# Weight splits one step behind their release, head sums one step later, and local tiles' buffers for the second dilated pair

## The chip, the cores and the metric
The kernel runs on one core of one Trainium2 chip. The metric is the device time of one execution in microseconds (us), from a median of three runs. TensorE (PE) does the matrix products, ScalarE (ACT) the activations and copies, VectorE (DVE) and GpSimd (POOL) the elementwise work, and SyncE (SP) only issues DMAs. Each engine has a queue of its own, in the order in which the program wrote it, with semaphore waits between the instructions; what stands behind a waiting instruction waits too.

## What is computed
Three transformer layers run in float32 over 512 tokens of width 1024 (layers two and three also carry 256 context tokens). Each has a modulation from a condition vector, a mixer and a gated feed-forward. The change concerns the first mixer, which has two kinds of attention heads on the same normalised input:

```python
qa = rms_norm(qa.reshape(b, s, NA_HEADS, HEAD_DIM), g_qa[l])       # 8 local heads, and ka
o_a = neighbourhood_attention(qa, ka, va, rpb[l])
qb = partial_rotary(rms_norm(qb.reshape(b, s, DIL_HEADS, HEAD_DIM), g_qb[l]), pos)  # 12, and kb
for g, (win, dil) in enumerate(DIL_CONFIGS):
    o_g, lse_g = dilated_window_attention(qb[:, :, sl], kb[:, :, sl], vb[:, :, sl], win, dil)
o_b = jnp.einsum('gbsh,gbshd->bshd', wts.astype(vb.dtype), jnp.stack(outs, axis=0))
merged = gate_a * (o_a @ w_proj_a[l]) + gate_b * (o_b @ w_proj_b[l])
```

The second mixer is grouped-query attention with the same kind of head norm and rotation, the third a gated recurrence.

## The kernel before
A planner in Python writes one long list of steps (`plan`), and every engine afterwards walks this list and issues its own part of each step. The order of steps is therefore the order in all queues.

**Weights.** A weight unit (`getunit`) is up to 128x1024 values, loaded by SP into one of three buffers `RAW`. Its `Split` step makes the two summands that the three-product scheme needs: ACT copies it rounded into `SHI` (line 2044), then POOL writes the remainder into `SLO` (line 2214; in the third mixer DVE does it, line 2274, at a step `SplitLow` put up to eight steps behind). `SHI` and `SLO` have three buffers too (`NSPL = 3`), so unit k can be split once unit k-3 has been read for the last time. `release(u, tok)` notes that moment and the place in the plan, `rel_at`, which is the index of the step right after the last product (`Chunk`). `with_splits` (line 370) puts the `Split` of unit k at `rel_at` of unit k-3, that is ahead of the step which follows the product. `load_order` takes a unit's place in SP's queue from the place of the split of the unit three before it, so it moves along.

**A projection job.** `na_qk(j, which)` and `dl_qk(j, g, which)` project one pair of heads: one unit, four chunks of six products each (two of the eight 128-row tiles of the input, three products each), with a yield behind each. Behind the fourth chunk comes `release`, then the square on ACT (`squared`, line 2067). The rest is a tail, which the job hands back: `headnorm` sums the squares over each head with a product on PE (line 2490), takes logarithm and exponential on ACT (2071, 2073), and multiplies on DVE (2317); for dilated heads `roped` follows with a permutation product on PE (2494), a product with the sines on DVE (2322), and cosine product and addition on POOL (2223, 2229), which writes the tile that the scores read.

**Pipelining.** `pipelined` (line 641) advances the tail of the job before by one yield after each chunk of the present one. When the present job ends, what is left of the tail before it is run through at once. A job with no chunk of its own (`after`, `qb2_cells`, `va_turned`, `dl_turned`, `dilated_loads`) ends at once, so it also drains the tail of the job in front of it, with no chunk between. `bgz` puts one tile of the modulation (a DVE reduction, line 2298) behind every fourth yield.

**Weaving.** `weave` (line 427) runs two sequences by clocks: a step of work w advances the attention's clock by (w+1)/0.6 and the dense list's by w+1, and the one that is behind goes next. A chunk counts 3072, a head sum or rotation 2048, the scores of a dilated pair 3072, its weighted sum 3584, a turn of three blocks 768. A sequence that waits for a name (`after`) takes up the other's clock when it goes on. `attention` works on pairs of items in four stages: scores of pair i, turn (transposes) of pair i-2, weighted sum of pair i-3; "na 3 done" is noted when pair 3 of the last local heads has been finished, which is two score steps into the dilated items.

**Tiles.** Local heads' projections lie in the four buffers of ring `qa`: heads j = 0 and 2 in the first two, 1 and 3 in the others. The first dilated pair has the six `qb` buffers. The second dilated pair's six tiles (`qb2`) lie over `va` and part of `qa`, and the dense list waits for them:

```python
dense += [dl_values(2), dl_qk(0, 2, "q"), dl_turned(2), dl_qk(0, 2, "k")]
dense += [after("na 3 done"), qb2_cells()]
dense += [dl_qk(1, g, w) for g in range(3) for w in "qk"]
dense += [early_gate(q, off) for q in range(2) for off in (0, 8)]
```

**Turnovers** (`turnover`, `sums`) end a layer's part: the last residual sums in halves of 256 tokens, squares and their running sum (ACT 2048, POOL 2219), then the next norm beside the first projections. There `release` comes ahead of a square.

Of the kernel before, what the change touches and what calls it, by code (L numbers as in the profile page):

```python
# [7 lines left out]
F32 = mybir.dt.float32  # L8
# [14 lines left out]
NSPL = 3  # L23
# [79 lines left out]
def seg(a, n):  # L103
    return ((a, n),)
# [137 lines left out]
def build_program(nc, t_in, out):  # L242
# [13 lines left out]
    def all_now():  # L256
        return [last[e] for e in "pavg" if e in last]
# [13 lines left out]
    def place(name, shape, dt, at):  # L271
        return nc.alloc_sbuf_tensor_at(name, shape, dt, offset=at)
# [25 lines left out]
    AR = base[0]  # L298
# [28 lines left out]
    def col(name, k=0):  # L327
        return COL[:, COLS[name][0] + k:COLS[name][0] + k + 1]


    units, adas = [], []
# [38 lines left out]
    def with_splits(steps):  # L370

        at, p = [], 0
        for u in units:
            if u.k < NSPL:
                p = first_splits[u.k]
            if u.k >= NSPL:
                p = max(p, units[u.k - NSPL].rel_at)
            assert p <= u.first_at, (u.key, p, u.first_at)
            u.split_at = p
            at.append((p, Split(u, units[u.k - NSPL].rel if u.k >= NSPL else None)))  # L380
            if u.on == "v":
                at.append((min(p + 8, u.first_at), SplitLow(u)))
        at.sort(key=lambda q: q[0])
        done, n = [], 0
        for i, st in enumerate(steps):
            while n < len(at) and at[n][0] <= i:
                done.append(at[n][1])
                n += 1
            done.append(st)
        return done  # L390
# [27 lines left out]
    def after(key):  # L418
        while key not in emitted:
            yield "wait"  # L420
# [246 lines left out]
    def headnorm(sq, bank, src, t_mm, T, gain, W, dst, t_dfree, views=None):  # L667

        s, t1 = sq
        b2 = take()  # L670
        r = W["r"].next()
        work[0] += 4 * T
        t2, t3, t4, t5 = tick("p_head"), tick("a_hln"), tick("a_hrs"), tick("v_head")
        dview, rview = views or (None, None)
        put(HNorm(s.ap[:, 0:T], b2.ap[:, 0:T], T, r.ap[:, 0:T], src, dst, dview, rview, gain, t1, b2.free, t2,
                  r.free, t3, t4, t_dfree, t5))
        s.free = [t2]
        give(b2, t3)
        r.free = [t5]
        give(bank, t5)  # L680
        return t5
# [291 lines left out]
    def marked(items, needs, name):  # L973
# [34 lines left out]
    W = arena({"va": (1, 4 * 512, F32, 4), "qa": (4, 512, F32, 4), "vb": (1, 3 * 4 * 256, F32, 4),  # L1008
               "qb": (6, 512, F32, 4), "mk": (1, 1536, F32, 4), "bi": (5, 384, F32, 4), "e": (4, 384, F32, 4),
               "f": (4, 512, F32, 4), "pt": (3, 768, F32, 4), "r": (2, 512, F32, 4), "o": (2, 128, F32, 4), "dg": (2, 128, F32, 4),  # L1010
               "m": (8, 8, F32, 4)}, [])
    qb2 = [place(f"qb2_{i}", [128, 512], F32, AR + 2048 * i)[:, :] for i in range(6)]
    oah = place("oah", [128, 4 * NT], F32R, HCh_at)
    oal = place("oal", [128, 4 * NT], F32R, HCl_at)
    obs = [[place(f"ob{n}{j}", [128, NT], F32R, XC_at + (4096, 0)[j] + 2048 * i)[:, :] for i, n in enumerate("hl")]
# [99 lines left out]
    qa_cells, qb_cells = {}, {}  # L1115

    def na_qk(j, which):
        u = getunit("w_in", ktiles(0, 8), seg(128 * j + (0 if which == "q" else 512), 128))
        b = take()
        t, = yield from proj(u, 0, [(b.ap, hl, hl_rdy, b.free)])  # L1120
        release(u, t)
        sq = squared(b.ap, t, NT, W)
        c = W["qa"].next()

        def tail():
            views = ("p (c r) -> p c r", "p (r c) -> p c r")
            yield
            c.rdy = [headnorm(sq, b, b.ap, t, NT, gq8 if which == "q" else col("gka"), W, c.ap, c.free, views)]
            qa_cells[(which, j)] = c
            yield  # L1130
            yield
            emitted.add(f"{which} {j}")

        yield
        return tail()
# [72 lines left out]
    def dl_qk(j, g, which):  # L1208
        u = getunit("w_in", ktiles(0, 8), seg((1536 if which == "q" else 1536 + 768) + 256 * g + 128 * j, 128))
        b = take()  # L1210
        t, = yield from proj(u, 0, [(b.ap, hl, hl_rdy, b.free)])
        release(u, t)
        sq = squared(b.ap, t, NT, W)

        def tail():
            yield
            c, n = qb_cells[(which, g, j)], W["f"].next()
            t5 = headnorm(sq, b, b.ap, t, NT, gqb8 if which == "q" else col("gkb"), W, n.ap, n.free)
            yield
            yield  # L1220
            c.rdy = [roped(n, t5, NT, perm1, W, c.ap, c.free, d_rope, "p (r s) -> p r s", "p (s r) -> p r s")]
            for _ in range(4):
                yield
            emitted.add(f"dilated {which} {g} {j}")

        yield
        return tail()
# [66 lines left out]
        gated[(q, off)] = (sg, t1)  # L1294
        yield

    def qb2_cells():
        na_done = all_now()
        for i, (g, w_) in enumerate([(g, w_) for g in range(3) for w_ in ("q", "k")]):
            qb_cells[(w_, g, 1)] = Cell(qb2[i], na_done)  # L1300
        return
        yield

# [5 lines left out]
    dense = []  # L1309
# [7 lines left out]
        dense += [dl_values(j)] if j < 2 else []  # L1317
    dense += [dl_qk(0, g, w) for g in range(2) for w in "qk"]
    dense += [dl_values(2), dl_qk(0, 2, "q"), dl_turned(2), dl_qk(0, 2, "k")]
    dense += [after("na 3 done"), qb2_cells()]  # L1320
    dense += [dl_qk(1, g, w) for g in range(3) for w in "qk"]
    dense += [early_gate(q, off) for q in range(2) for off in (0, 8)]
    dense += [some(bg, 32)]
    first_out = lambda it, o, t: (na_make if "t" in it else dl_make)(it, o, t)
# [106 lines left out]
    W = arena({"hh": (6, 512, F32R, 4), "hl": (6, 512, F32R, 4), "f": (4, 512, F32, 4), "r": (2, 512, F32, 4)}, blk, c_at)  # L1431
# [43 lines left out]
    for c in W["r"].cells:  # L1475
# [14 lines left out]
    W = arena({"f": (4, 512, F32, 4), "r": (2, 512, F32, 4), "hh": (2, TT, F32R, 4), "hl": (2, TT, F32R, 4),  # L1490
               "q": (2, TT, F32, 4), "k": (2, TT, F32, 4), "v": (1, 6 * 256, F32, 4), "e": (4, TT, F32, 4),
               "pt": (2, 2 * TT, F32, 4), "o": (2, 128, F32, 4), "dg": (2, 128, F32, 4), "m": (8, 8, F32, 4)}, blk, c_at)
# [88 lines left out]
    heads, dense = [], []  # L1581
# [29 lines left out]
    W = arena({"hh": (6, TT, F32R, 4), "hl": (6, TT, F32R, 4), "f": (4, TT, F32, 4), "r": (2, 512, F32, 4)}, all_now(), c_at)  # L1611
    hid = hids(W)

    def with_mask(main):
        for i, _ in enumerate(main):
            if i == 20:
# [12 lines left out]
    W = arena({"v": (1, 6 * 256, F32, 4), "xy": (4, 2 * TT, F32, 4), "kk": (2, TT, F32, 4), "q": (2, NT, F32, 4),  # L1629
               "sg": (2, NT, F32, 4), "t": (2, TT + 1, F32, 4), "ek": (1, TT + 1, F32, 4), "eq": (1, NT, F32, 4),  # L1630
               "R": (1, 2 * NT, F32, 4), "A": (1, NT, F32, 4), "kt": (1, TT + 1, F32, 4), "S": (4, 128, F32, 4),
               "f": (1, NT, F32, 4), "r": (1, NT, F32, 4), "hh": (2, NT, F32R, 4), "hl": (2, NT, F32R, 4),
               "pe": (4, 8, F32, 4), "de": (4, 8, F32, 4)}, blk)
# [329 lines left out]
    dense = []  # L1963
# [17 lines left out]
    W = arena({"hh": (6, NT, F32R, 4), "hl": (6, NT, F32R, 4), "f": (4, NT, F32, 4), "r": (2, 512, F32, 4)}, all_now())  # L1981
# [683 lines left out]
```

## Time and profile before

| | us |
|---|---|
| median of three runs | 2824.49 |
| the three runs | 2822.01 to 2826.79 |
| the profiled execution | 2823.09 |
| its span, first to last instruction | 2820.7 |
| PE busy in it | 2635.6 |
| first mixer | about 64 to 387 |
| second mixer | about 953 to 1335 |
| third mixer | about 1950 to 2412 |

The mean granted TensorE clock was 0.976 of full speed. In a timeline row stand the start, the duration, the engine and source line, the operation with output and inputs, the count, and in brackets how long the engine had been idle before it and for what. PE works through a pipeline: matmuls of 128x512 last 0.39 us each but start 0.23 us apart, so the starts are what one counts with.

### The profile page before, as it was taken

What the parts mean: (1) busy time and instruction counts of PE and PEld (TensorE: products, weight loads), DVE (VectorE), ACT (ScalarE), POOL (GpSimd) and SP (SyncE); (2) the same over time, 40 slices, a digit from 0 to 9 for tenths busy, and PEclk for the clock granted to TensorE, in tenths of its full rate; (3) what the DMA queues carried; (4) which work ended last, traced back from release to release, by engine and by line L of the source; (5) the groups of instructions that cost most, each with busy time, mean ns of one, the idle gap of its engine ahead of it and who ended that gap; (6) DMA issues with size and microseconds to landing.
All of it is one profiled execution on the core that took longest, in us unless ns stands there. A gap on an engine that the chain in (4) does not pass through costs nothing. (4 is left out here: it accounts for less than half of the span.)

```text
span 2820.7 us, 39428 instructions
## 1 busy us (share of the span) xinstructions
PE 2635.6 (93%) x15242; PEld 2204.5 (78%) x15242; DVE 1564.4 (55%) x2439; ACT 1101.7 (39%) x2033; POOL 982.2 (35%) x561
## 2 busy tenths in 40 slices
PE   5998989899999899998899999999899998899998
PEld 3765678788888767766788888888788887788887
DVE  5445247654564445656666555556768677632224
ACT  3453442332322455555412112225555546422222
POOL 2335534444544311222333232332222122344444
PEclk9998999999999999999999999999999999899999
DMA  6643224343333100001233333321111110132222
GB/s 253 217 161 135 71 84 145 127 142 132 131 134 127 37 21 20 27 27 47 75 132 135 112 113 130 117 90 43 51 51 53 53 58 34 46 104 97 97 97 75
DMA packets 81608, 267.83 MB, mean 95 GB/s; under 512 B 8720, under 2 KB 16528, under 8 KB 81424
## 3 DMA queue, kind: packets, MB, share of 16 engines
q1 hardware_dynamic: 78000, 257.59, 26.3%
q10 hardware_dynamic: 3136, 6.42, 0.6%
q8 instruction: 122, 2.00, 0.3%
q0 software_dynamic: 288, 1.31, 0.1%
q14 instruction: 62, 0.51, 0.1%
HBM read 260.57 MB, written 4.72 MB: 94 GB/s over the span
## 5 line engine op out<-in xcount | busy, mean ns | idle before, releaser
L2214 POOL TENSOR_TENSOR SLO<-RAW,SHI 128x1024 fp32r<-128x1024 f32 (+1 forms) x291 | 708.4, 2437 | 1136.4 <-ACT SHI L2044 1130.9
L2044 ACT ACTIVATE SHI<-RAW 128x1024 fp32r<-128x1024 f32 (+1 forms) x335 | 345.4, 1035 | 1031.4 <-PE PS L2484 1024.1
L2482 PE MATMUL PS<-HLh,SHI 128*128 128x512 f32 (+1 forms) x1800 | 708.8, 394 | 21.3 <-DVE HLl L2288 11.4
L2483 PE MATMUL PS<-HLl,SHI 128*128 128x512 f32 (+1 forms) x1800 | 683.2, 380 | 0.0
L2484 PE MATMUL PS<-HLh,SLO 128*128 128x512 f32 (+1 forms) x1800 | 683.0, 379 | 0.0
L2482 PEld LDWEIGHTS PS<-HLh,SHI 128*128 128x128 f32 x1800 | 344.9, 192 | 94.0 <-issue 30.4
L2484 PEld LDWEIGHTS PS<-HLh,SLO 128*128 128x128 f32 x1800 | 344.0, 191 | 64.2
L2483 PEld LDWEIGHTS PS<-HLl,SHI 128*128 128x128 f32 x1800 | 345.3, 192 | 60.6 <-issue 5.6
L2482 PE MATMUL PS<-hh,SHI 128*128 128x512 f32 (+1 forms) x1016 | 365.3, 360 | 11.9 <-DVE XL L2360 7.9
L2484 PE MATMUL PS<-hh,SLO 128*128 128x512 f32 (+1 forms) x1016 | 356.7, 351 | 0.0
L2483 PE MATMUL PS<-hl,SHI 128*128 128x512 f32 (+1 forms) x1016 | 355.0, 349 | 0.0
L2360 DVE SCALAR_TENSOR_TENSOR XL<-PS,MOD,XL 128x512 f32<-128x512 f32 (+1 forms) x328 | 211.7, 667 | 179.2 <-PE PS L2484 179.1
L2367 DVE TENSOR_TENSOR hl<-f,hh 128x512 fp32r<-128x512 f32 x88 | 165.0, 1875 | 122.8 <-ACT hh L2113 122.8
L2482 PEld LDWEIGHTS PS<-hh,SHI 128*128 128x128 f32 x1016 | 192.3, 189 | 49.7 <-issue 11.7
L2365 DVE TENSOR_TENSOR f<-f,PS 128x512 f32<-128x512 f32 x88 | 54.3, 616 | 303.7 <-PE PS L2484 285.1
L2484 PEld LDWEIGHTS PS<-hh,SLO 128*128 128x128 f32 x1016 | 192.3, 189 | 27.1
L2483 PEld LDWEIGHTS PS<-hl,SHI 128*128 128x128 f32 x1016 | 192.4, 189 | 26.5
L2482 PE MATMUL PS<-HCh,SHI 128*128 128x256 f32 x560 | 168.0, 300 | 12.1 <-POOL SLO L2214 6.1
L2298 DVE CUSTOM_DVE_ANT_0 ADA<-ADA,cb,COL 128x1024 f32<-128x1024 f32 x96 | 177.2, 1846 | 0.0
L2483 PE MATMUL PS<-HCl,SHI 128*128 128x256 f32 x560 | 162.4, 290 | 0.0
L2484 PE MATMUL PS<-HCh,SLO 128*128 128x256 f32 x560 | 162.2, 290 | 0.0
L2298 DVE CUSTOM_DVE_ANT_0 cdump<-ADA,cb,COL 128x1024 f32<-128x1024 f32 x96 | 138.1, 1439 | 12.0 <-DMA ADA<-in_k_w 12.0
(259 smaller groups left out, 3949.9 us busy)
## 6 DMA issues: line engine op xcount, KB each, us to landing
RAW<-in_k_w SPq DMA_DIRECT2D x317, 512.0 KB, 3.5
ADA<-in_k_w SPq DMA_DIRECT2D x132, 512.0 KB, 4.3
early<-in_k_w SPq DMA_DIRECT2D x12, 512.0 KB, 18.6
RAW<-in_k_w SPq DMA_DIRECT2D x18, 256.0 KB, 2.6
XL<-in_xT ACTq DMA_DIRECT2D x4, 512.0 KB, 13.7
bi<-in_k_bias SPq DMA_DIRECT2D x16, 128.0 KB, 3.8
out<-XL SPq DMA_DIRECT2D x16, 128.0 KB, 1.8
bi<-in_k_bias SPq DMA_DIRECT2D x8, 192.0 KB, 4.1
```

The costliest lines, as they stand in the source:

```text
L2044: eng.activation(u.hi, u.w, ACT.Copy).then_inc(S["a_hi"], 1)
L2214: eng.tensor_tensor(u.lo, u.w, u.hi.bitcast(F32), ALU.subtract).then_inc(S["g_lo"], 1)
L2298: eng.tensor_tensor_reduce(w if j == n - 1 else st.dump, w, c, 1.0, st.bias, ALU.mult, ALU.add, st.mod[:, j:j + 1]).then_inc(S["v_ada"], 1)
L2360: eng.scalar_tensor_tensor(out=st.x, in0=st.src, scalar=st.gate, in1=st.x, op0=ALU.mult, op1=ALU.add).then_inc(S["v_res"], 1)
L2365: eng.tensor_tensor(st.f, st.f, st.src, ALU.mult).then_inc(S["v_up"], 1)
L2367: eng.tensor_tensor(st.lo, st.f, st.hi.bitcast(F32), ALU.subtract).then_inc(S["v_ulo"], 1)
L2482: eng.matmul(st.out, lh, rh, start=st.first and j == 0, stop=False)
L2483: eng.matmul(st.out, lh, rl, start=False, stop=False)
L2484: i = eng.matmul(st.out, ll, rh, start=False, stop=st.last and j == n - 1)
```

## The change
Three parts. The `Split` of unit k goes one step behind the place where it was, but never behind its first use. The tails of `na_qk` and `dl_qk` have one more yield ahead of the head sum. The second dilated pair's tiles go, for groups 0 and 1, into the buffers of the local tiles, as soon as local heads 2 and 3 have been scored; only group 2 takes new buffers over `va`, once the local heads are done. The one wait ahead of the six jobs becomes three waits, one ahead of each group.

```diff
@@ with_splits
             if u.k >= NSPL:
-                p = max(p, units[u.k - NSPL].rel_at)
+                p = max(p, min(units[u.k - NSPL].rel_at + 1, u.first_at))
@@
-    qb2 = [place(f"qb2_{i}", [128, 512], F32, AR + 2048 * i)[:, :] for i in range(6)]
+    qb2 = [place(f"qb2_{i}", [128, 512], F32, AR + 2048 * i)[:, :] for i in range(2)]
@@ na_qk, tail (one yield more)
             yield
+            yield
              c.rdy = [headnorm(sq, b, b.ap, t, NT, gq8 if which == "q" else col("gka"), W, c.ap, c.free, views)]
@@ dl_qk, tail (one yield more)
         def tail():
+            yield
             yield
             c, n = qb_cells[(which, g, j)], W["f"].next()
@@
-    def qb2_cells():
-        na_done = all_now()
-        for i, (g, w_) in enumerate([(g, w_) for g in range(3) for w_ in ("q", "k")]):
-            qb_cells[(w_, g, 1)] = Cell(qb2[i], na_done)
+    def qb2_cells(g):
+
+        free = all_now()
+        for i, w_ in enumerate("qk"):
+            local = W["qa"].cells[2 * g + i] if g < 2 else Cell(qb2[i], free)
+            qb_cells[(w_, g, 1)] = Cell(local.ap, local.free)
@@
-    dense += [after("na 3 done"), qb2_cells()]
-    dense += [dl_qk(1, g, w) for g in range(3) for w in "qk"]
+    for g, done in enumerate(("na 2 scored", "na 3 scored", "na 3 done")):
+        dense += [after(done), qb2_cells(g)] + [dl_qk(1, g, w) for w in "qk"]
```

## Rows read from the trace of the kernel before

**Rows 1.** The page, its first part: busy time, share, instructions of each engine
```profile
PE 2635.6 (93%) x15242; PEld 2204.5 (78%) x15242; DVE 1564.4 (55%) x2439; ACT 1101.7 (39%) x2033; POOL 982.2 (35%) x561
```

**Rows 2.** PE's waits, whole span: line, releaser, total us, times, longest
```profile
PE PS L2490 <- ACT f L2067: 13.5, 8, 1.7
...
PE PS L2482 <- POOL SLO L2214: 11.7, 6, 4.0
...
PE PS L2482 <- DVE SLO L2274: 1.0, 1, 1.0
```

**Rows 3.** Timelines of ACT and PE around one drained tail
```profile
104.87 1.06 ACT L2044 ACTIVATE SHI<-RAW 128x1024 fp32r<-128x1024 f32 x1 [0.17 <-PE PS L2484]
105.83 0.58 ACT L2067 ACTIVATE f<-PS 128x512 f32<-128x512 f32 x1
107.63 0.69 ACT L2071 ACTIVATE r<-PS,SMALL 128x512 f32<-128x512 f32 x1 [1.22 <-PE PS L2490]
...
106.47 1.13 PE L2490 MATMUL PS<-f,CONST 128*128 128x512 f32 x2 [1.69 <-ACT f L2067]
```

**Rows 4.** PE's timeline where the dense list waits for "na 3 done"
```profile
250.95 0.39 PE L2484 MATMUL PS<-HLh,SLO 128*128 128x512 f32 x1
...
256.72 2.07 PE L2494 MATMUL PS<-f,CONST 128*128 128x512 f32 x2 [2.57 <-DVE f L2317]
263.30 2.93 PE L2502 MATMUL PS<-qb,qb 64*128 64x512 f32 x12 [4.51 <-POOL qb L2229]
...
273.54 0.55 PE L2509 MATMUL PS<-CONST,e 128*128 128x128 f32 x3 [1.25 <-ACT pt L2085]
```

**Rows 5.** PE and DVE timelines, a covered tail of a dilated job
```profile
329.35 1.02 PE L2490 MATMUL PS<-f,CONST 128*128 128x512 f32 x2
...
331.60 0.39 PE L2482 MATMUL PS<-HLh,SHI 128*128 128x512 f32 x1
...
332.98 1.02 PE L2494 MATMUL PS<-f,CONST 128*128 128x512 f32 x2
...
331.80 0.75 DVE L2317 SCALAR_TENSOR_TENSOR f<-PS,COL,r 128x512 f32<-128x512 f32 x1 [4.33 <-ACT r L2073]
```

**Rows 6.** ACT, POOL and PE timelines ahead of the second dilated pair's first scores
```profile
333.23 1.06 ACT L2044 ACTIVATE SHI<-RAW 128x1024 fp32r<-128x1024 f32 x1 [1.47 <-PE PS L2484]
...
338.10 2.10 POOL L2229 TENSOR_TENSOR qb<-f,r 128x512 f32<-128x512 f32 x1
...
340.25 2.93 PE L2502 MATMUL PS<-qb,qb 64*128 64x512 f32 x12 [4.86 <-POOL qb L2229]
```

**Rows 7.** PE's timeline, and granted clock (last but two column), at a drained dilated tail
```profile
243.15 1.23 PE L2494 MATMUL PS<-f,CONST 128*128 128x512 f32 x2 [2.23 <-DVE f L2317]
243.71 1.09 PE L2482 MATMUL PS<-HLh,SHI 128*128 128x512 f32 x1
...
244.00:246.00 2.00, 2.00 (x6) 0.51 1.00 327
```

**Rows 8.** POOL and PE timelines in two turnovers
```profile
918.84 1.62 POOL L2219 TENSOR_TENSOR r<-r,f 128x256 f32<-128x256 f32 x2 [1.84 <-ACT f L2048]
920.41 2.35 POOL L2214 TENSOR_TENSOR SLO<-RAW,SHI 128x1024 fp32r<-128x1024 f32 x1
...
922.82 0.39 PE L2482 MATMUL PS<-HCh,SHI 128*128 128x256 f32 x1 [2.71 <-POOL SLO L2214]
...
1920.95 0.58 PE L2482 MATMUL PS<-HCh,SHI 128*128 128x256 f32 x1 [3.36 <-POOL SLO L2214]
```

**Rows 9.** DVE and ACT timelines behind a dilated pair's scores
```profile
266.26 0.96 DVE L2330 CUSTOM_DVE_ANT_0 e<-PS,mk 128x768 f32<-128x768 f32 x1 [4.96 <-PE PS L2502]
...
268.19 0.92 ACT L2079 ACTIVATE e<-e,m 128x768 f32<-128x768 f32 x1
```

**Rows 10.** The line 2367 by itself: ns min/median/max, first and last start, forms
```profile
L2367 DVE TENSOR_TENSOR hl<-f,hh x88: 424/2472/2483, 575.0 to 2777.8; 128x512 fp32r<-128x512 f32 x66, 128x256 fp32r<-128x256 f32 x22
```

**Rows 11.** PE's timeline in the second mixer
```profile
1325.37 0.44 PE L2515 MATMUL PS<-dg,CONST 128*64 128x128 f32 x4 [1.77 <-ACT dg L2089]
```

## The prediction
> **What bounds the kernel.** I read the first part of the page, then PE's waits, then the timelines around the longest. PE is busy 2635.6 of the 2820.7 us [rows 1]; in the feed-forward stages it never stops. So an edit is worth something only where PE stands, 185 us in all, or runs at the lower clock. The change can reach three kinds of such places. (a) The head sum waits for the square on ACT, 8 times, 13.5 us [rows 2]. (b) In the stall for "na 3 done" PE waits 2.57, 4.51 and 1.25 us and works at half rate in between [rows 4]. (c) PE waits for low halves, 11.7 us on POOL and 1.0 us on DVE [rows 2]. The sums below are differences, made against the profiled 2823.09 us (span 2820.7 and 2.4 around it), which lies 1.4 below the median of 2824.49. I add the net to the median. About 0.2%, 5.6 us, is what a measurement can tell from no change.
>
> **Part 1, splits one step later.** Where a projection job ends, the split (1.06 us) stands on ACT ahead of the square: it starts at 104.87, the square at 105.83, and PE's head sum at 106.47 after 1.69 us idle [rows 3]. With the order turned round the square starts 0.96 us earlier. The split then runs beside the head-sum product, and the logarithm, which starts 1.16 us behind the head sum [rows 3], still finds ACT free. Seven of the eight waits of [rows 2] have a split ahead of the square (the eighth, in the second mixer, has none): 7 x 0.96 = **6.7 us less**.
> The moved step also moves POOL's low half and the load that waits for it. In the feed-forwards the split now stands behind an activation, at most some 2 us, and PE comes to the unit two units later (2 x 4 chunks of 1.38 us, 331.60 to 332.98 [rows 5], 11 us); cost nothing, and if that cover were gone, up to 2 us a unit. SP's queue keeps its order but for ties. In two turnovers there is no cover: PE already waits for a low half, 2.71 and 3.36 us [rows 8], and the split falls behind one square and POOL's running sum, 1.62/2 = 0.8 us. **1.7 us more**. In the second mixer a split ahead of a copy delays a wait such as the 1.77 us one [rows 11]: between 0 and 1.0 less, I take **0.5 less**, since the usual order there (split, square, logarithm) ends at the same time either way. In the third mixer `SplitLow` moves a step on DVE; the nearest row is the 1.0 us wait for such a low half [rows 2], so I bound it by -2 and +2 and take 0.
>
> **The port rule.** The low halves of the feed-forwards take 2.47 us in the median, 0.42 at least [rows 10]; they run beside POOL's `SLO`, and with the split behind the high half they would mostly come first. PE waits for none of them, so the sum gets nothing. The Trainium skill (SBUF — State Buffer, section "SBUF: two separate sides") says that DVE, with two SBUF inputs, and a reading GpSimd instruction take a shared port pair as an exclusive lock, whoever starts first. By that rule nearly all 88 would be freed, over 100 us of DVE time as an estimate, but still not a us on PE unless DVE set an end.
>
> **Part 2, head sums a step later.** All seven waits above are at drained tails, where an empty job follows; one more yield changes nothing there. Where the tail is covered, the head sum had no wait before and has none now. What changes is its distance to the rotation. Of a dilated job's tail only four calls fall beside chunks; the head sum moves from behind chunk 2 to behind chunk 3, and the rotation stays behind chunk 4. Head sum at 329.35, DVE's product ends at 331.80 + 0.75 = 332.55, so the rotation can start 3.2 us behind the head sum; two chunks took until 332.98, one ends at 331.60, 2.25 us behind it [rows 5]. So a wait of 1.0 us arises per covered dilated tail without attention in between: `dl_qk(0,1,q)` and `(1,2,q)`, **2.0 us more**. The tail of `(1,2,k)` ends in the scores of the second pair. There the chain is split 333.23, low half, cosines, sums until 340.20, scores 340.25 [rows 6]; the gate's copy, now ahead of the split, puts it 0.6 later, **0.6 more**. The bank held a chunk longer leaves two for the turns for that chunk; from 0 to 1 us, I take 0.
>
> **Part 3, the stall.** Gone: the turn's wait of 1.25 us [rows 4]; and one chunk, 1.38 us at full rate, goes into the 4.51 us in front of the scores. **2.6 us less** (if attention's waits are only pushed on, 1.4; if its slow stretch gets shorter too, 5). The 2.57 and most of the 4.51 stay: the two empty jobs after `dl_qk(0,2,k)` drain its tail just as the wait did, and the slow clock stays with them. The 12 us in which attention ran alone are mostly work, which is done anyway.
> What is new: `after` and `qb2_cells` also stand behind `dl_qk(1,0,k)` and `(1,1,k)`, and drain their tails, which were covered. By the planner's clocks, with 0 where attention is released: the head sum of (1,0,q) comes at 15,365, chunk 4 of (1,0,k) at 20,486, the drain runs from 23,559 to 29,712; attention's pieces are at 21,775 (a turn), 23,057 (scores of the third pair) and only then 28,179. So on PE scores, rotation, head sum and rotation stand in a row. ACT's exponentials come ahead of the logarithm: from the end of the scores (266.26) to the end of the second exponential (268.19 + 0.92) is 2.85 us [rows 9], logarithm to DVE's end another 2.05 (3.2 less 1.16), less 1.3 for the rotation and the head sum on PE (0.87, which is 2.25 less a chunk, and two products of 0.23): 3.6 us idle. "na 3 done" comes at 23,057, long before the list asks. Attention is blocked from 55,507 (it needs the second pair), the second drain starts at 56,348 with nothing beside it: 3.2 less two products of 0.23 = 2.7 us idle. After 1.69 and 2.23 us of idling near each other the granted clock was 0.51, the lower level, and 24 products took 7.5 us, 1.6 more than at full rate [rows 4, 7]. I count one such fall for the two drains, bounds none and two. 3.6 + 2.7 + 1.6 = **7.9 us more**.
>
> **Sum.** -6.7 + 1.7 - 0.5 + 2.0 + 0.6 - 2.6 + 7.9 = +2.4: 2824.5 + 2.4 = **2827**.
>
> **Rivals.**
> Drains covered, faster: if attention pieces lie between the head sum and the rotation in both new drains, or the chip's queues lag the plan by a piece, the 7.9 fall to about 1, and the shorter wait may also keep the clock up at 243.71 [rows 7], 1.6 less. 2.4 - 6.9 - 1.6 = -6.1: 2818. For it: the clocks miss by a few hundred only; against it: within a drain a yield costs the dense list 1.
> DVE relieved: if DVE sets PE's pace at only four of the 88 places where a low half gets up to 2.05 us shorter (2.47 less 0.42 [rows 10]), 8.2 us go: 2819. For it: the low half is the last step of a hidden tile. Against it: no row shows PE waiting for one. The port rule above would let this happen.
> Slower, by the clock: idle gaps of 1.0 us and more now stand in nearly every dilated tail. If the clock falls at both drains (+1.6) and in the pure stretch ahead of the second pair's scores (+1.6), and the other covered dilated tails (three with attention between) wait 1 us each as well, +3, that is 2.4 + 6.2 = 8.6: 2833. It decides once more than 3.2 us come on top of the sum. For it: one fall after 3.9 us of idling in 5 [rows 7].
> That the change doesn't do what it says: part 3 would not if the names it waits for came too late; but both local pairs are scored before the dense list has done its first pair's last group, at 250.95 [rows 4]. Under 0.02, and in the forecast.
>
> **Chances.** Forecast and near it (within 0.2%) 0.47; drains covered 0.17 and DVE relieved 0.07, with small other gains 0.25 for faster; slower 0.28. The range reaches from 2813, the first rival with the third mixer's 2 us and the drains' last us, to 2837, the slower one with 2 us of the third mixer, a bank wait and late turnovers. The likeliest case's own range is 2819 to 2830.
>
> **What would show it.** In the changed kernel the square at job ends starts before the split and the seven waits of 1.69 read about 0.7. No attention runs alone between 258 and 275; chunks stand ahead of the scores. New waits of the rotation (line 2494) on DVE: about 3.6 and 2.7 us at two places between 280 and 320, and about 1.0 where only one chunk lies behind the head sum. The turnovers' waits for `SLO` grow by 0.8. I am wrong if the two new drains show no wait above 1 us, if the waits on squares stay at 1.69, or if spans behind 1950 differ by more than 2 us.

## The result and the profile after

| | us |
|---|---|
| before, median of 6 runs | 2824.55 (2822.01 to 2826.79) |
| after, median of 6 runs | 2834.05 (2832.89 to 2836.30) |
| ratio | 1.0035, 95% interval 1.0024 to 1.0047 |
| the profiled execution of after, and its span | 2836.30, 2834.4 |

The kernel became 9.5 us slower. The forecast was 2827; the time lies in the range, but it is what the rival "slower, by the clock" gave (2833), not the forecast. The profiled execution is the longest of the six, so single differences below are good to some 2 us in sum.

Three views of after, which answer to [rows 1], [rows 2] and [rows 10]. First the page's first part:

```profile
PE 2647.1 (93%) x15242; PEld 2210.5 (78%) x15242; DVE 1527.2 (54%) x2439; ACT 1102.8 (39%) x2033; POOL 973.4 (34%) x561
```

PE's waits over the span (line, releaser, total, times, longest):

```profile
PE PS L2498 <- DVE f L2321: 21.1, 14, 4.2
PE PS L2486 <- POOL SLO L2218: 13.5, 6, 4.6
...
PE PS L2506 <- DVE qa L2321: 5.9, 2, 3.0
...
PE PS L2494 <- ACT f L2071: 5.3, 8, 0.7
```

The feed-forwards' low halves by themselves (ns min/median/max):

```profile
L2371 DVE TENSOR_TENSOR hl<-f,hh x88: 426/693/2431, 584.5 to 2791.0; 128x512 fp32r<-128x512 f32 x66, 128x256 fp32r<-128x256 f32 x22
```

Three things stand here. The waits for the square fell from 13.5 to 5.3 us, 1.0 us at nearly every one of the eight (the forecast had seven of them). PE's waits for DVE grew: those of the rotations' product (L2498) from 11.8 to 21.1, those for `qa` from 2.3 to 5.9. And the median low half of the feed-forwards fell from 2.47 to 0.69 us, while the time rose.

Where the loss lies is read from PE's first product with `SHI` behind the first mixer, which is the same product in every kernel:

| kernel | that product starts at, us | against before |
|---|---|---|
| before | 404.75 | |
| after | 414.64 | +9.9 |
| part 1 alone | 399.08 | -5.7 |
| part 2 alone | 409.66 | +4.9 |
| part 3 alone | 410.72 | +6.0 |
| parts 1 and 3 without drains | 391.79 | -13.0 |

So 9.9 of the 13.7 us by which the spans of the two profiled executions differ arise before 415 us. Another 6.0 come between there and the turnover ahead of the third mixer, and 2.2 are given back behind it; the part on the last tries takes these up. (The other kernels of the table come below.) After's timelines of ACT at the first new drain, and of PE at the first drain, which before had too [rows 4], and at both new ones:

```profile
289.63 0.94 ACT L2083 ACTIVATE e<-e,m 128x768 f32<-128x768 f32 x1 [0.33 <-DVE m L2334]
290.56 0.92 ACT L2083 ACTIVATE e<-e,m 128x768 f32<-128x768 f32 x1
291.48 0.67 ACT L2075 ACTIVATE r<-PS,SMALL 128x512 f32<-128x512 f32 x1
...
260.46 2.08 PE L2498 MATMUL PS<-f,CONST 128*128 128x512 f32 x2 [4.22 <-DVE f L2321]
266.27 2.93 PE L2506 MATMUL PS<-qb,qb 64*128 64x512 f32 x12 [1.17 <-POOL qb L2233]
293.65 1.98 PE L2498 MATMUL PS<-f,CONST 128*128 128x512 f32 x2 [3.14 <-DVE f L2321]
321.32 2.08 PE L2498 MATMUL PS<-f,CONST 128*128 128x512 f32 x2 [2.39 <-DVE f L2321]
```

And PE's granted clock (the number behind the bracket) right behind those two drains, in windows of after:

```profile
293.60:297.00 3.40, 3.35 (x13) 0.53 0.00 0
321.00:324.00 3.00, 2.67 (x4) 0.51 0.52 175
```

The drains came where the plan had them: two exponentials ahead of the logarithm, 3.14 us of wait for the forecast's 3.6, and 2.39 for 2.7. But the clock fell to its lower level, 1.2 GHz, behind both, and not behind one.

The rest is at the local heads. DVE and POOL of after near 115 us, and PE's waits at 89, 119 and 160:

```profile
114.83 3.29 DVE L2302 CUSTOM_DVE_ANT_0 ADA<-ADA,c,COL 128x1024 f32<-128x1024 f32 x1 [2.85 <-DMA ADA<-in_k_w]
118.05 1.06 DVE L2321 SCALAR_TENSOR_TENSOR qa<-PS,COL,r 128x512 f32<-128x512 f32 x1
...
114.66 2.38 POOL L2218 TENSOR_TENSOR SLO<-RAW,SHI 128x1024 fp32r<-128x1024 f32 x1 [4.38 <-ACT SHI L2048]
...
89.06 1.65 PE L2506 MATMUL PS<-qa,qa 64*128 64x384 f32 x4 [2.24 <-DVE m L2334]
119.17 0.75 PE L2506 MATMUL PS<-qa,qa 64*128 64x256 f32 x4 [2.92 <-DVE qa L2321]
160.17 0.79 PE L2506 MATMUL PS<-qa,qa 64*128 64x256 f32 x4 [2.97 <-DVE qa L2321]
```

Before, the same place looked like this (DVE):

```profile
117.28 1.07 DVE L2317 SCALAR_TENSOR_TENSOR qa<-PS,COL,r 128x512 f32<-128x512 f32 x1 [5.93 <-ACT r L2073]
118.28 1.27 DVE L2298 CUSTOM_DVE_ANT_0 ADA<-ADA,c,COL 128x1024 f32<-128x1024 f32 x1
```

A modulation tile's reduction used to stand behind the head product; now it stands ahead of it. It waits at DVE's head for its own load until 114.83, and then takes 3.29 us instead of 1.27, beside POOL's low half. ACT has the logarithm and the exponential done at 116.2, and DVE is taken until 118.05. That tile is not in the prediction at all.

### The profile page after: what moved, and what is told of

The parts are those of the page before. It is cut to its first block and busy times, and to the rows that moved or that the text cites. A ratio compares the mean times of both kernels' runs of the same rounds, so it can differ in the third digit from the quotient of the medians.

```text
span 2834.4 us, 39340 instructions
## 1 busy us (share of the span) xinstructions
PE 2647.1 (93%) x15242; PEld 2210.5 (78%) x15242; DVE 1527.2 (54%) x2439; ACT 1102.8 (39%) x2033; POOL 973.4 (34%) x561
## 5 line engine op out<-in xcount | busy, mean ns | idle before, releaser
L2486 PE MATMUL PS<-HLh,SHI 128*128 128x512 f32 (+1 forms) x1800 | 708.5, 394 | 18.7 <-DVE HLl L2292 10.6
L2486 PE MATMUL PS<-hh,SHI 128*128 128x512 f32 (+1 forms) x1016 | 365.8, 360 | 11.9 <-DVE XL L2364 7.9
L2486 PEld LDWEIGHTS PS<-hh,SHI 128*128 128x128 f32 x1016 | 192.7, 190 | 49.7 <-issue 11.8
L2302 DVE CUSTOM_DVE_ANT_0 ADA<-ADA,cb,COL 128x1024 f32<-128x1024 f32 x96 | 199.5, 2078 | 0.0
L2117 ACT ACTIVATE hh<-f 128x512 fp32r<-128x512 f32 x88 | 50.6, 575 | 295.4 <-DVE f L2369 295.1
L2302 DVE CUSTOM_DVE_ANT_0 cdump<-ADA,cb,COL 128x1024 f32<-128x1024 f32 x96 | 146.3, 1524 | 9.0 <-DMA ADA<-in_k_w 9.0
## 6 DMA issues: line engine op xcount, KB each, us to landing
XL<-in_xT ACTq DMA_DIRECT2D x4, 512.0 KB, 13.7
```

Source lines behind the costliest of these rows:

```text
L2117: eng.activation(st.hi, st.f, ACT.Copy).then_inc(S["a_uhi"], 1)
L2302: eng.tensor_tensor_reduce(w if j == n - 1 else st.dump, w, c, 1.0, st.bias, ALU.mult, ALU.add, st.mod[:, j:j + 1]).then_inc(S["v_ada"], 1)
L2486: eng.matmul(st.out, lh, rh, start=st.first and j == 0, stop=False)
```

## The theory and the rivals

**Theory.** The three parts don't add up. The extra yields change two things besides the head sum's place: the count by which `bgz` gives out the modulation tiles (every fourth step; each drained tail is now a step longer), and so the place of these tiles on DVE. When part 1 lets PE run ahead, the tile that moved forward has not been loaded yet, and all that is queued behind it on DVE is late. The two new drains come on top, each with a clock fall.
**Rival A.** Part 1 gives nothing by itself: what the square saves is lost at the head product, since POOL's low half now runs beside it.
**Rival B.** The drains are all of it.
**Rival C.** The long waits come from the later head sums themselves, not from the tile.

## One part at a time

The first: before, with part 1 alone.

```diff
-                p = max(p, units[u.k - NSPL].rel_at)
+                p = max(p, min(units[u.k - NSPL].rel_at + 1, u.first_at))
```

> The kernel before with the change's first part alone: splits are placed one step behind the release of their buffers, nothing else is changed. Theory (the early split is a gain of its own, and what ate it is the modulation tile that the second part puts ahead of the head product): 7 tails lose 1.0 us of wait each, the turnovers cost 1.7, so 5 us less than before: 2819.5 us (2817 to 2822); the scores behind the first and the third tail wait 1.1 to 1.2 us for the head product, as before. Rival (what the square no longer waits for comes back at the head product, because the low halves' pass on GpSimd then runs beside it): those scores wait 2.5 to 3 us, and the time is 2824.5 (2823 to 2826). Second rival (the turnovers cost more than the squares give): 2827 or more.

Measured: 2815.04 (2812.11 to 2818.64), ratio 0.9971 (0.9961 to 0.9982), before in the same series 2823.82: 8.8 us less. From its trace, PE's waits on the square and on `qa`:

```profile
PE PS L2490 <- ACT f L2067: 5.5, 8, 0.7
...
PE PS L2502 <- DVE qa L2317: 2.3, 2, 1.2
```

and DVE's timeline at the tile near 85 us:

```profile
83.88 0.42 DVE L2330 CUSTOM_DVE_ANT_0 e<-PS,bi 128x256 f32<-128x256 f32 x1
85.39 1.28 DVE L2298 CUSTOM_DVE_ANT_0 ADA<-ADA,c,COL 128x1024 f32<-128x1024 f32 x1 [1.08 <-DMA ADA<-in_k_w]
```

Rival A falls: the waits for `qa` are as before, and the squares' gain stays. The tile waits for its load here too, but behind the scores' evictions, where nobody waits for it. The product behind the mixer starts at 399.08, 5.7 us earlier, for the 5 us expected in all. By the medians 3 us more came behind it; in the profiled execution, the shortest of the seven, it is 5.4, with a granted clock of 0.98 in the third mixer's stretch (1970 to 2450) for 0.95 of before. The seven executions of this kernel spread over 6.5 us with mean clocks from 0.974 to 0.979, so how much of these 3 us is the change's stays open.

The second: before, with part 2 alone (one more yield ahead of both head sums).

```diff
         def tail():
             ...
+            yield
             yield
```

> The kernel before with the change's second part alone: the head sum of both kinds of tail is given out one step later, nothing else. Theory (each drained tail shifts the count by which the background gives out modulation tiles, and a tile now stands on VectorE ahead of a head product): the scores near 119 and 160 us wait about 1.8 us longer each, three short waits for banks come to 2 to 3 us, two dilated tails come to 1.0 each less or more: 5 us more than before, 2829.5 (2828 to 2832). Rival (the loss of the whole change lies in the new drains alone): 2824.5 (2823 to 2826), and both waits stay at 1.1 to 1.2 us.

Measured: 2828.71 (2823.61 to 2829.81), ratio 1.0015 (1.0006 to 1.0024): 4.9 us more by the medians, 4.2 by the ratio, as the size was expected, but not by those rows. PE's timeline:

```profile
118.52 0.70 PE L2504 MATMUL PS<-qa,qa 64*128 64x256 f32 x4 [1.14 <-DVE qa L2319]
158.54 0.70 PE L2504 MATMUL PS<-qa,qa 64*128 64x256 f32 x4 [1.52 <-DVE qa L2319]
...
306.06 1.13 PE L2496 MATMUL PS<-f,CONST 128*128 128x512 f32 x2 [0.83 <-DVE f L2319]
```

and DVE's at the two tiles that have moved:

```profile
113.39 1.28 DVE L2300 CUSTOM_DVE_ANT_0 ADA<-ADA,c,COL 128x1024 f32<-128x1024 f32 x1 [1.96 <-DMA ADA<-in_k_w]
...
154.36 3.12 DVE L2300 CUSTOM_DVE_ANT_0 ADA<-ADA,c,COL 128x1024 f32<-128x1024 f32 x1 [3.25 <-DMA ADA<-in_k_w]
```

At 119 and 160 PE waits 1.14 and 1.52, little longer than the 1.12 and 1.17 of before, though the tiles have moved. They wait for their loads at DVE's head here too (1.96 and 3.25), and the second takes 3.12 us; but the loads come early enough against the head products, at 117.39 and 157.42, so that only the second is late, and by little. What costs is the rotations' wait of 0.83, six times (220.84 and five from 306 to 339), and two waits for a bank near 200 and 213, 0.86 and 0.89.

The third: before, with part 3 alone.

```diff
-    dense += [after("na 3 done"), qb2_cells()]
-    dense += [dl_qk(1, g, w) for g in range(3) for w in "qk"]
+    for g, done in enumerate(("na 2 scored", "na 3 scored", "na 3 done")):
+        dense += [after(done), qb2_cells(g)] + [dl_qk(1, g, w) for w in "qk"]
```

> The kernel before with the change's third part alone: the second dilated pair's tiles go to local tiles' buffers as these come free, so its projections start earlier and are parted by two jobs without steps. Theory (the two jobs drain a tail each, with 3.1 and 2.4 us of wait for VectorE's rope behind the exponentials, and the granted clock falls behind both): 2.6 us saved at the last drain, 5.5 us of waits and 1.6 us twice of slow clock: 6 us more than before, 2830.5 (2828 to 2833). Rival (earlier projections fill the idle time of TensorE elsewhere and pay for the drains): 2824.5 (2822 to 2826).

Measured: 2831.10 (2829.86 to 2833.18), ratio 1.0028 (1.0018 to 1.0039): 7.3 more; the drains' waits here are 4.00 and 2.30 us, and the clock falls behind both as in after (0.50 from 290 to 293, 0.70 from 319 to 322). The rival, with earlier projections paying for the drains, falls.

The three by themselves sum to -8.8 + 4.9 + 7.3 = +3.4, close to the +2.4 of the prediction. The whole change cost 9.5. So a further 6 us lies in how the parts act on one another, and parts 1 and 2, run together without part 3, show it (the other two pairs were not run with the drains in):

> The kernel before with the first and the second part of the change, without the third. The first part alone gave 2815.0, the second alone 2828.7, before 2823.8. Theory (the two don't add up: only when TensorE runs ahead, by the first part, and the tile stands one place forward, by the second, is the tile's transfer too late): 8.8 saved, 4.9 lost, and 5.8 us lost besides near 89, 119 and 160: 2825.7 (2824 to 2828). Rival (they add up): 2819.9 (2818 to 2822).

Measured: 2828.91 (2823.46 to 2833.55), ratio 1.0017 (1.0008 to 1.0026). By the sum it would be 2819.9; it is 9.0 above it, more than the theory's 5.8. (In the profiles the product behind the mixer starts at 414.59, 10.6 above the sum.) With part 3 added the whole is 5.1 above it, for 7.3 on the kernel before. Its DVE and PE timelines:

```profile
88.21 1.28 DVE L2300 CUSTOM_DVE_ANT_0 ADA<-ADA,c,COL 128x1024 f32<-128x1024 f32 x1 [3.47 <-DMA ADA<-in_k_w]
...
90.25 1.65 PE L2504 MATMUL PS<-qa,qa 64*128 64x384 f32 x4 [3.27 <-DVE m L2332]
121.59 0.70 PE L2504 MATMUL PS<-qa,qa 64*128 64x256 f32 x4 [2.93 <-DVE qa L2319]
```

and its granted clock behind 90 us:

```profile
91.00:93.00 2.00, 2.00 (x9) 0.50 0.92 344
93.00:95.00 2.00, 2.00 (x12) 0.50 0.06 21
```

DVE waits 3.47 us for the tile's load, PE 3.27 us for the exponentials' maxima behind it, and the clock falls to 0.50 until past 95 us. Behind the wait of 2.97 at 161.09 it falls too, but behind the one of 2.93 at 121.59 it does not, though it did in after behind nearly the same wait. The first two rows are of this kernel, the last two of after:

```profile
121.00:123.00 2.00, 1.41 (x10) 1.00 1.00 356
161.00:163.00 2.00, 1.91 (x6) 0.52 0.90 350
...
119.00:121.00 2.00, 1.83 (x9) 0.68 0.95 378
121.00:123.00 2.00, 2.00 (x12) 0.50 0.99 407
```

The waits are 3.27 and twice 1.8 longer, and the half clock costs some 3 us at the first and 1.7 at the third: 12 in this execution, more than the 9.0. From 230 to 245 us the clock was 0.77 in part 1 alone and 1.00 here, 3.4 us the other way; but that difference need not be the change's, as the kernel with no drain at all shows below. Neither part alone shows a wait at 89 or one of nearly 3 us at 119 and 160. The row at 114.83 of after shows the second half of it: the reduction takes 3.29 us beside POOL's `SLO` (114.66 to 117.04). The Trainium skill (SBUF — State Buffer, section "SBUF: two separate sides") has DVE and GpSimd share a port pair as an exclusive lock; the row agrees with it: `SLO` still had 2.21 us to go when the reduction was issued, 2.21 and 1.28 are 3.49, and `SLO` itself took no longer than before (2.38 for 2.36). The load is not what makes it slow: of the two rows of part 2 alone above, both waited for their loads, and the one at 154.36 took 3.12 beside an `SLO` with 2.04 us to go, the one at 113.39, with POOL idle until 114.38, 1.28.

## The tile's place or the late head sum

After, with the extra steps left out of `bgz`'s count, so that the tiles keep their pace.

```diff
+            if got == "more":
+                yield
+                continue
             i += 1
             if i % every == 0:
                 next(bg, None)
...
-            yield
+            yield "more"
             yield
```

> The changed kernel, with the added steps left out of the count by which the background gives out modulation tiles, so that these stand on VectorE where they stood before against the head products and the exponentials' work. Theory (a modulation tile that has moved one place forward waits at VectorE's head for its own transfer, and TensorE then waits for what is queued behind it: 2.24 us at 89, 1.8 more at 119, 1.8 more at 160, 1.65 more at 260): these go, 7.5 us less than the changed kernel: 2826.5 us (2824 to 2829). Rival (the longer waits are the late head sums' own, a projection further on): 2834 (2832 to 2836) with 2.9 us of wait at the scores near 119 and 160 still there.

Measured: 2827.63 (2824.73 to 2830.60), ratio to before 1.0013 (1.0004 to 1.0022): 6.4 less than after, and no execution of the one overlaps one of the other. PE's timeline:

```profile
88.56 0.92 PE L2509 MATMUL PS<-qa,qa 64*128 64x384 f32 x4 [2.35 <-DVE m L2337]
115.38 0.70 PE L2509 MATMUL PS<-qa,qa 64*128 64x256 f32 x4 [1.14 <-DVE qa L2324]
153.08 0.70 PE L2509 MATMUL PS<-qa,qa 64*128 64x256 f32 x4 [1.19 <-DVE qa L2324]
```

The waits at 119 and 160 are back at 1.14 and 1.19: there the tile's place was the cause, and rival C falls for them. Twice 1.8 of waits and 1.6 of clock are 6.8, close to the 6.4. The wait at 89 stays (2.35): DVE's row shows a tile waiting for its load until 86.52, still ahead of the scores' evictions. The count is not what puts it there; likely the later head sum also shifts attention's pieces against the dense steps, which was not tried. So this edit closes one of the ways by which a tile gets ahead. That the load's lateness is the cause is read from DVE's rows; no kernel with an earlier load was run.

## The two new drains

After, with `after` and `qb2_cells` of groups 1 and 2 run inside the projection's job that follows, so that no job without steps drains a tail.

```diff
+    def freed_then(done, g):
+        yield from after(done)
+        for _ in qb2_cells(g):
+            pass
+        return (yield from dl_qk(1, g, "q"))
+
-    for g, done in enumerate(("na 2 scored", "na 3 scored", "na 3 done")):
-        dense += [after(done), qb2_cells(g)] + [dl_qk(1, g, w) for w in "qk"]
+    dense += [after("na 2 scored"), qb2_cells(0)] + [dl_qk(1, 0, w) for w in "qk"]
+    for g, done in ((1, "na 3 scored"), (2, "na 3 done")):
+        dense += [freed_then(done, g), dl_qk(1, g, "k")]
```

> The changed kernel, with the wait for the local scores and the naming of the cells put inside the job of the projection that follows, for the second and third group, so that the two new drains are gone; all else as changed. Theory (the drains and the clock that falls behind them are most of the loss): the waits of 3.1 and 2.4 us near 293 and 321 go, and the stretches of half clock behind them: 8.7 us less than the changed kernel, 2825.4 (2823 to 2828). Rival (VectorE, busy with exponentials' scaling, masks and modulation tiles there, is late by as much wherever the rope stands, and TensorE waits for it at the scores of the second pair instead): 2832 to 2835, with a wait near 350 us longer by 5 us or more.

Measured: 2825.91 (2818.10 to 2829.22), ratio to before 1.0001 (0.9992 to 1.0010). Against after that is 8.1 us (9.6 by the ratios to before), where the prediction's term was 7.9: 5.5 us of waits and the two clock falls. The scores of the second pair wait 4.21 us, the same as in after; what came up in the drains' place is one wait of a rotation, 0.83, and 1.7 us more at the first dilated scores (2.87 for 1.17). Rival B falls too, in its strict form: the drains are 8.1 of the loss, and the change without them is still worth nothing, since part 2 has eaten what part 1 gave.

## Parts 1 and 3, without part 2

The same with part 2 taken out: splits later, cells early, no new drain.

> The kernel before with the first part of the change and the third, the wait and the cells of the second and third group set inside the job of the projection, so that they drain nothing; the second part is left out. Theory: the 2815.0 of the first part alone, less the 2.6 us that the third part gives at the first dilated scores: 2812.4 (2810 to 2815). Rival (VectorE, with the ropes of the second pair among the exponentials' work, makes TensorE wait elsewhere by at least as much): 2817 to 2820.

Measured: **2810.02** (2809.31 to 2815.62), ratio to before 0.9958 (0.9946 to 0.9971): 14 us faster than before, 24 faster than after. Part 2 alone parts this kernel from the last one, and there it costs 15.9 us by the medians (13.2 by the means; 15.4 at the product behind the mixer), where on the kernel before it cost 4.9. Its PE timeline:

```profile
113.42 0.70 PE L2512 MATMUL PS<-qa,qa 64*128 64x256 f32 x4 [1.14 <-DVE qa L2327]
255.40 1.57 PE L2512 MATMUL PS<-qb,qb 64*128 64x512 f32 x12 [1.97 <-POOL qb L2239]
328.00 2.29 PE L2512 MATMUL PS<-qa,qa 64*128 64x512 f32 x6 [5.28 <-POOL qb L2239]
```

and its granted clock from 260 us:

```profile
260.00:275.00 15.00, 14.08 (x90) 1.00 0.33 105
```

The same window of before had a clock of 0.74, and of part 1 alone 0.92. A chunk now stands in front of the first dilated scores (their wait 1.97, not 4.51 [rows 4]), and with less idle time there PE is back at full clock 260 to 275. Part 3 without drains is worth 5.0 against part 1 alone by the medians, 3.8 by the means, with overlapping intervals. The prediction had 2.6, and 5 for the case that "its slow stretch gets shorter too"; the rows are those of that case, the size is between the two.

What the late head sums cost without any moved count: the fourth kernel (no new drains) with the old pace of tiles.

> The changed kernel without the two new drains (2825.9) and with the added steps left out of the count for the modulation tiles: of the second part only the later head sums are left. Theory (the tile's place and the late head sums each cost by themselves): as on the changed kernel, 6.4 less, 2819.5 (2817 to 2822), so that the later head sums cost 9.5 against the 2810.0 of the kernel that differs from this one by them alone. Rival (nearly all that the second part costs is the modulation tile's place): 2812 (2810 to 2815).

Measured: 2821.33 (2816.60 to 2826.20), ratio to before 0.9990 (0.9981 to 0.9999): 4.6 less than with the new pace, 11.3 more than without part 2 (3.2 and 10.0 by the means). So the later head sums are the larger share of the 15.9. The tile's pace is the smaller one, and not clear of noise here, as the intervals of the two kernels overlap (0.9981 to 0.9999 and 0.9992 to 1.0010). Of the later head sums' cost PE's rows show the wait at 89 (2.52 us, with the clock down behind it), four rotations' waits of 0.83, and two waits for banks. They were not tried apart. These waits sum to 7.6 us, while the first rotation's wait near 250 is 3.0 shorter (2.22 for 5.20), and the clock from 80 to 110 was 0.89 for 1.00, worth 3.3 us. That is 7.9 of the 11.9 us by which the product behind the mixer is later (403.65 for 391.79); the rest stays open.

## Two more tries that gave nothing

The drain that before has near 251 us taken out as well, by treating group 0 like the others.

```diff
-    dense += [after("na 2 scored"), qb2_cells(0)] + [dl_qk(1, 0, w) for w in "qk"]
-    for g, done in ((1, "na 3 scored"), (2, "na 3 done")):
+    for g, done in ((0, "na 2 scored"), (1, "na 3 scored"), (2, "na 3 done")):
```

> As the kernel with splits and cells and without the two new drains, and the cells of the first group are set inside its projection's job too, so that the drain that the kernel before has near 251 to 257 us is gone as well: the next projection lies between the head sum and the rope there. Theory (that drain is a wait of 4.0 us and a wait of 4.5 us at the first dilated scores, one of which is covered): 4 us less than the kernel with that drain, 2808.5 (2806 to 2812). Rival (the scores still wait for GpSimd's rope, now further on, and the projection only moves): within 1.5 us of it.

Measured: 2814.51 (2810.88 to 2816.01), ratio 0.9965 (0.9953 to 0.9978), not faster than the 2810.02. PE's timeline at the first dilated scores of this kernel:

```profile
259.74 2.93 PE L2511 MATMUL PS<-qb,qb 64*128 64x512 f32 x12 [6.24 <-POOL qb L2238]
```

and its granted clock to the mixer's end:

```profile
200.00:396.02 196.02, 169.71 (x986) 0.94 0.28 90
```

The rotation's wait of 5.2 is gone and the scores' wait has grown from 1.97 to 6.24: the projection moved, and the chain rotation, POOL's sum, scores is as long as before. The rival was right on the chain. The two kernels' executions overlap (2809.31 to 2815.62 and 2810.88 to 2816.01), so they can't be told apart.

The profiles differ by 4.2 us at the product behind the mixer, and most of that is not the edit's. Ahead of 236 us both walk the same steps with the same waits, 0.69 at the head sum and 2.23 at the rotation; behind that, with PE at work without a gap in both, the clock was 1.00 in the kernel with the drain and 0.50 in this one. First with the drain, then without:

```profile
237.00:239.00 2.00, 2.00 (x11) 1.00 0.97 353
```

```profile
237.00:239.00 2.00, 2.00 (x5) 0.50 0.95 334
```

From 230 to 245 the mean was 1.00 and 0.77, 3.4 us. So whether the clock falls behind a given wait can differ between two executions of the same steps, and a clock fall seen in one profile only need not be the kernel's own.

The fastest kernel with part 1 kept to the first mixer (`mixed` is the plan's length behind its weave):

```diff
-                p = max(p, min(units[u.k - NSPL].rel_at + 1, u.first_at))
+                p = max(p, min(units[u.k - NSPL].rel_at + (u.first_at < mixed), u.first_at))
```

> The kernel with splits and cells and without the two new drains (2810.0), with the split one step later only for weights whose first projection lies in the first mixer; elsewhere the split stands where it stood before. Theory (at the turnovers a split one step later makes GpSimd's low half late: 0.9 us more near 913 and 1.2 more near 1912, and 2.4 instead of 1.2 near 1353): those waits are 2.7, 3.4 and 1.2 again, 3.3 us less: 2806.7 (2804 to 2809). Rival (the later splits of the second mixer save as much there as the turnovers cost, or the clock takes it): 2810 (2808.5 to 2812).

Measured: 2814.13 (2808.69 to 2815.47), ratio 0.9957 (0.9945 to 0.9970), the same as 0.9958. The same product of the third mixer's turnover, first without and then with this edit:

```profile
1912.44 0.58 PE L2492 MATMUL PS<-HCh,SHI 128*128 128x256 f32 x1 [4.57 <-POOL SLO L2224]
```

```profile
1907.05 0.58 PE L2493 MATMUL PS<-HCh,SHI 128*128 128x256 f32 x1 [3.35 <-POOL SLO L2225]
```

It comes 5.4 us earlier, 5.2 of which arise behind the first mixer, and 4.3 of these are three waits (3.57 for 1.73, 2.37 for 1.16, 4.57 for 3.35). But the spans of the two kernels differ by 1.4 us only, so 4 us are given back from there to the end. The profiles of all twelve kernels bear both out:

| | splits as before (4 kernels) | splits a step later (8 kernels) |
|---|---|---|
| from the product behind the first mixer to this one, us | 1514.0 to 1519.1, mean 1516.2 | 1517.6 to 1522.2, mean 1520.8 |
| from this one to the end, us | 898.2 to 899.8, mean 899.1 | 893.0 to 897.5, mean 895.9 |

So the later splits cost 4.6 us up to the turnover ahead of the third mixer and give 3.2 back in the third mixer and behind it. The gain is spread: a wait of 1.84 for `S` near 2010 is gone and one for `HLl` near 2430 is 3.40 for 4.49; the rest wasn't placed. Cost and gain cancel to within what the times can tell.

## Why the prediction was half right

- **Squares, -6.7.** Right on the mechanism, a little low: all eight waits fell, from 13.5 to 5.3 us. The prediction says that the eighth, in the second mixer, has no split ahead of its square; ACT's row of before has one at 951.51, the square at 952.47, and PE's wait at 953.10 fell from 1.69 to 0.69 as the others did.
- **Turnovers +1.7, second mixer -0.5, third mixer 0.** The two waits for `SLO` grew by 0.9 and 1.2, for the forecast's 0.8 each; a third, for `HCl` near 1360, was missing from the sum (1.17 before, 2.37 in seven of the eight kernels with later splits, though 1.95 with part 2 or 3 alone, too). Over twelve profiles the stretch up to the turnover ahead of the third mixer costs 4.6 and the rest gives 3.2. The third mixer's 0 was wrong in size, and the sign that the prediction names for it, spans behind 1950 that differ by more than 2 us, is there (2.2 in after, 3.9 in four of the kernels). The net of about 1 is as in the sum only because the two errors cancel.
- **Part 2, +2.6.** This is the step that failed: "at drained tails ... one more yield changes nothing there". The wait for the square it does leave alone. But a drained yield is a step of the dense list, steps are what gives out the modulation tiles, and a tile that isn't loaded blocks all of DVE. Part 2 cost 4.9 alone and 15.9 on the kernel where PE ran ahead. The count is the smaller share of the latter (3 to 5 us); the larger is that of the later head sums themselves, of which about two thirds was found in PE's rows. The rotations' waits were sized well (0.83 for 1.0) but came at more tails; the banks, taken as 0, gave 0.86 and 0.89.
- **The stall, -2.6.** Right on the wait (1.97 for 4.51 at the scores), low on the clock: 3.8 to 5.0 without drains.
- **The new drains, +7.9.** 8.1 measured: waits a little shorter (3.14 and 2.39 for 3.6 and 2.7), and two falls of the clock for one.
- **DVE relieved.** The low halves did shrink, from 165.0 to 97.8 us in sum (88 times, mean 1875 to 1111 ns), 67 us where the prediction estimated over 100, and the two reductions over `cb` took 315.3 to 345.8 together. PE gained nothing from it, as the prediction had it: from the product behind the first mixer to that of [rows 11] in the second took 920.6 us before and 922.7 after.
- **The rival "slower, by the clock"** came near the time (2833) mostly by luck. Of its three terms the fall of the clock at both drains came true. The fall ahead of the second pair's scores is no loss of the change's: the clock fell there in before too (0.56 from 339 to 344, and 0.68 from 350 to 355 in after). Of its three further rotations' waits one came. The interaction of parts 1 and 2, the larger part of the surprise, was in no rival.
- **The sum.** Measured singly, the parts gave -8.8, +4.9 and +7.3, where the prediction's terms for them are -5.5, +2.6 and +5.3; that both sums are near (+3.4 and +2.4) is luck, since the errors cancel. What failed besides is the sum's assumption that the parts add. The time lies in the range because the range is 24 us wide, not because this was foreseen.

## What to carry to other kernels

Before adding a step to a generator, list all that count its steps, not only what stands behind it: a background task paced by steps moves too, and an instruction that waits for its own transfer blocks everything behind it on its in-order engine. Test the parts of a change singly and in pairs; here one part was worth -8.8, another turned that into +4.5, and leaving that one out (with the two waits put inside the next job) gave the fastest kernel. A drain can cost the half clock behind it on top of its wait. And don't put a clock fall that one profile shows down to the edit before you have seen it in several kernels that share the place.

## What the runs showed of the hardware

The granted clock fell to 0.53, 0.51 and 0.50, the 1.2 GHz level, behind idle gaps of 3.14, 2.39 and 2.92 us of after, and in before it stayed at 1.00 behind the gap of 1.12 at 118.41; here is that last window:

```profile
118.40:120.40 2.00, 1.99 (x15) 1.00 1.04 405
```

So a wait of the head product that grows from 1.1 to 2.9 us can cost about 3.5 and not 1.8. It doesn't always: the clock stayed at 1.00 behind a wait of 2.93 (121.59, parts 1 and 2 together), one of 2.81 (89.37, the change without the two new drains) and one of 2.35 (88.56, old pace), while it fell to 0.50 behind the 2.24 at the same place in after (89.06). The length of the wait alone doesn't tell. The reduction over 1024 columns took 1.28 us alone and 3.29 or 3.12 us beside POOL's low half. Executions of one kernel differed by up to 11 us (2818.10 to 2829.22, the kernel without the two new drains), with mean clocks from 0.973 to 0.980.
